# Splitting one chunk's weights pass by pass among the index scores, and another's between the two halves of the inputs

## The reference

```python
h = rmsnorm(x, g_norm_mix[l]) * (1.0 + sc1[:, None, :]) + sh1[:, None, :]
proj = jnp.einsum('bsd,de->bse', h, w_in)          # 4688 columns
qa, ka, va, qi, ki, wi, qb, kb, vb, gb = jnp.split(proj, cuts, axis=-1)
...
# index scores of the sparse attention, 16 heads of 64
dots = jnp.einsum('bqhe,bse->bqhs', qib, k_idx, preferred_element_type=jnp.float32)
score = jnp.einsum('bqh,bqhs->bqs', wb.astype(jnp.float32), jax.nn.relu(dots * IDX_DIM ** -0.5))
_, sel = lax.top_k(score, k_top)                   # 256 keys of each query
...
y_b = retention(qb, kb, vb, gb, positions)         # the second group of heads
```

## Time and profile before

| what | value |
|---|---|
| time, median of 3 runs | 1697.28 us (1694.88 to 1703.69) |
| profiled execution, its own time | 1695.42 us |
| its span, first to last instruction | 1693.5 us |
| PE busy | 1473.0 us, 87% of the span |
| DVE, ACT, POOL busy | 1128.7, 913.3, 279.7 us |
| mean granted TensorE clock | 0.930 |

### The profile page before, as it was taken

How to read it: one execution, slowest core, us unless ns; L and a number is a source line. 1 busy time by engine, 2 the same in 40 slices (tenths; PEclk the granted TensorE clock), 3 DMA queues, 4 the chain that set the end, 5 groups by cost and what they waited for, 6 DMA issues and landing times.

```text
span 1693.5 us, 21565 instructions
## 1 busy us (share of the span) xinstructions
PE 1473.0 (87%) x7406; PEld 1150.1 (68%) x7406; DVE 1128.7 (67%) x1500; ACT 913.3 (54%) x1228; POOL 279.7 (17%) x208
## 2 busy tenths in 40 slices
PE   3899998999999898888899943999999999999940
PEld 2587444888887786456666732788888888888830
DVE  6632778662257983434444345899999999999936
ACT  4320576878994112323444401777777777777711
POOL 0000100240000000200000001223232232332126
PEclk9899989999999998689999966999999999999975
DMA  9198532223324234112211105999999999999847
GB/s 370 50 332 313 200 147 106 90 77 120 109 92 131 69 118 169 65 62 65 86 51 44 38 25 193 401 396 398 404 404 396 394 399 399 394 396 401 347 165 275
DMA packets 102566, 368.01 MB, mean 217 GB/s; under 512 B 11232, under 2 KB 23648, under 8 KB 77792
## 3 DMA queue, kind: packets, MB, share of 16 engines
q1 hardware_dynamic: 74208, 291.58, 45.1%
q10 hardware_dynamic: 17024, 41.95, 6.5%
q0 software_dynamic: 11264, 33.57, 5.5%
HBM read 306.24 MB, written 69.21 MB: 222 GB/s over the span
## 4 chain that ended last, share of the span: by engine, by line
PE 75%; DVE 12%; ACT 4%; issue 3%; DMA 3%; POOL 3%; SPq 0%; DVEq 0%; POOLq 0%; ACTq 0%
PE PS L1627 19%; PE PS L1629 19%; PE PS L1628 19%; PE PS L1728 3%; PE PS L1751 2%; PE PS L1931 2%; PE PS L1837 2%; PE PS L1824 2%; DMA WK<-in_w_ada 1%; DVE wlo L1550 1%; POOL raw L741 1%; DVE WK L1049 1%; PE PS L1713 1%; PE PS L1684 1%; PE PS L1906 1%
## 5 line engine op out<-in xcount | busy, mean ns | idle before, releaser
L1550 DVE TENSOR_TENSOR wlo<-raw,whi 128x2048 fp32r<-128x2048 f32 x192 | 435.8, 2285 | 33.4 <-ACT whi L962 32.9
L962 ACT ACTIVATE whi<-raw 128x2048 fp32r<-128x2048 f32 x192 | 363.9, 1914 | 116.2 <-DVE WK L1569 80.7
L1627 PE MATMUL PS<-whi,xhi 128*128 128x512 f32 x512 | 203.6, 398 | 7.3 <-DVE wlo L1550 6.5
L1629 PE MATMUL PS<-whi,xlo 128*128 128x512 f32 x512 | 200.9, 392 | 0.0
L1628 PE MATMUL PS<-wlo,xhi 128*128 128x512 f32 x512 | 199.9, 390 | 0.0
L853 ACT ACTIVATE KV<-ACC,WK 128x1024 int8<-128x1024 f32 (+4 forms) x160 | 147.5, 925 | 29.9 <-DVE WK L1185 27.3
L1627 PE MATMUL PS<-KVR,BIGR 128*128 128x512 f32 x320 | 127.6, 399 | 5.9 <-DVE KVR L1111 5.9
L1629 PE MATMUL PS<-KVR,BIGR 128*128 128x512 f32 x320 | 125.4, 392 | 0.0
L1628 PE MATMUL PS<-KVR,BIGR 128*128 128x512 f32 x320 | 125.0, 391 | 0.0
L702 POOL COPY wcol<-tw 128x1 f32 (+1 forms) x32 | 63.0, 1970 | 373.9 <-DVE WK L1587 373.9
L1627 PEld LDWEIGHTS PS<-whi,xhi 128*128 128x128 f32 x512 | 96.9, 189 | 27.6 <-issue 5.7
(11 more groups left out here) (326 smaller groups left out, 2966.0 us busy)
## 6 DMA issues: line engine op xcount, KB each, us to landing
raw<-in_w_gate SPq DMA_DIRECT2D x64, 1024.0 KB, 7.2
raw<-in_w_up SPq DMA_DIRECT2D x64, 1024.0 KB, 7.8
raw<-in_w_down SPq DMA_DIRECT2D x64, 1024.0 KB, 7.2
y_dram<-zero ACTq DMA_DIRECT2D x8, 3072.0 KB, 11.3
WK<-in_w_ada POOLq DMA_DIRECT2D x16, 1024.0 KB, 7.4
y_dram<-WK ACTq DMA_DIRECT2D x32, 512.0 KB, 6.6
KV<-in_w_in SPq DMA_DIRECT2D x5, 2048.0 KB, 10.4
KV<-in_x SPq DMA_DIRECT2D x16, 512.0 KB, 5.2
```

What stands on the lines that cost most here:

```text
L962: nc.scalar.activation(whi[:, slot], raw[:, q], ACT.Copy).then_inc(G("m_hi"), 1)
L1550: V.tensor_tensor(wlo[:, slot], raw[:, q], whi[:, slot].bitcast(F32), ALU.subtract)\
L1627: mm(out_, x_hi, w_hi, start=first, stop=False)
L1629: return mm(out_, x_lo, w_hi, start=False, stop=final)
```

## The change

Chunk 0's high passes on ACT now stand between the copy of the first keys and `hidden_high(1)`. Chunk 2's high passes are put one each behind the relus of u = 48, 52, 56 and 60; its low passes on DVE one each ahead of the sums of u = 50, 54, 58 and 62, each behind the wait for that unit's relu. The block of four low passes behind the memsets is gone. No instruction is added or taken out, and PE, POOL and SP have the orders they had.

```diff
--- before.py
+++ after.py
@@ -35,6 +35,7 @@
 TBL = MAX_ITEMS + 2
 NEG_SCORE = -3.0e38
 
+SPLIT_AT = 4
 STEP_SPEND = 5.0
 TAKEN = -3.4e38
 NEG_LOGIT = -1.0e30
@@ -783,11 +784,11 @@
 
 
 
-            def split_high(n):
+            def split_high(n, part=None):
 
                 act.wait_ge(G(f"ld_w{n % 3}"), 16 * (n // 3 + 1))
                 raw_, _, hi = W[n]
-                for k in range(0, KD, 2):
+                for k in range(0, KD, 2) if part is None else (2 * part,):
                     own.go(A(hi[:, k:k + 2], raw_[:, k:k + 2], ACT.Copy), G("w_hi"))
 
             def hidden_high(half):
@@ -815,10 +816,10 @@
             hidden_high(0)
             act.wait_ge(G("key_pe"), 1)
             own.go(A(keys_turned[0:KEYS, 0:512], PS[0:KEYS, 6, :], ACT.Copy), G("key_act"))
+            split_high(0)
             hidden_high(1)
             act.wait_ge(G("key_pe"), 2)
             own.go(A(keys_turned[0:KEYS, 512:1024], PS[0:KEYS, 7, :], ACT.Copy), G("key_act"))
-            split_high(0)
             act.wait_ge(G("key_pe"), 3)
             own.go(A(keys.rearrange("p (b t) c -> p b t c", b=2),
                      PS[:, 6:8, 0:4 * KEYS].rearrange("p b (t c) -> p b t c", t=4), ACT.Copy), G("key_act"))
@@ -837,8 +838,8 @@
                     act.wait_ge(G("sc_acc"), u - 2)
                 own.go(A(WA["R"][:, u % 3, 0:K], PS[:, b:b + 2, :].rearrange("p b c -> p (b c)")[:, 0:K], ACT.Relu),
                        G("sc_relu"))
-                if u == NU // 2:
-                    split_high(RETAIN)
+                if u >= NU // 2 and u % SPLIT_AT == 0 and u < NU // 2 + 4 * SPLIT_AT:
+                    split_high(RETAIN, (u - NU // 2) // SPLIT_AT)
 
             for group in range(2):
                 act.wait_ge(G("late_used"), LATE_STEPS)
@@ -1103,10 +1104,10 @@
                 v = tmp.rearrange("p (h c) -> p h c", h=8)[:, :, 0:16].rearrange("p h (a d) -> p h a d", a=2)
                 own(rotate_part(v, t, 8), G("a_rot"))
 
-            def split_low(n):
+            def split_low(n, part=None):
 
                 raw_, lo, hi = W[n]
-                for k in range(0, KD, 2):
+                for k in range(0, KD, 2) if part is None else (2 * part,):
                     dve.wait_ge(G("w_hi"), 4 * n + k // 2 + 1)
                     own.go(V.tensor_tensor(lo[:, k:k + 2], raw_[:, k:k + 2], hi[:, k:k + 2].bitcast(F32), ALU.subtract),
                            G("w_lo"))
@@ -1154,6 +1155,8 @@
                 acc = ACC[:, ACC_OFF[i]:ACC_OFF[i] + K]
                 R = WA["R"][:, u % 3, 0:K]
                 dve.wait_ge(G("sc_relu"), u + 1)
+                if u >= NU // 2 + 2 and (u - 2) % SPLIT_AT == 0 and u < NU // 2 + 2 + 4 * SPLIT_AT:
+                    split_low(RETAIN, (u - 2 - NU // 2) // SPLIT_AT)
                 if h == 0:
                     own(V.tensor_scalar(acc, R, wsc[:, i, h:h + 1], None, ALU.mult), G("sc_acc"))
                 else:
@@ -1168,8 +1171,6 @@
             own(V.memset(sel_flip, 0))
             for group in range(2):
                 own(V.memset(sel_try[:, 3 * group:3 * group + 3], -2 ** 31), G(f"sel_try{group}"))
-            split_low(RETAIN)
-
             def narrow(n):
 
                 bit, group = 31 - n // 2, n % 2
```

## The result

The changed kernel takes 1682.64 us (median of 6 runs, 1681.62 to 1686.32) where the kernel before takes 1697.82 (median of 6, 1694.88 to 1703.69) in the same comparison. The ratio is 0.9909 with a 95% interval from 0.9894 to 0.9924, so 15.2 us are gained, from 12.9 to 18.0 by the interval. The forecast was 1684.9 and a gain of 12.4. In a later comparison the same kernel gave 0.9923 [0.9906, 0.9941], 13.1 us. The forecast range holds both medians; the second interval includes the forecast gain, the first just doesn't.

The account below looks back on a forecast made before the run. The prediction took PE to bound the kernel (75% of the chain that ended last, DVE 12%), with three waits for weight passes. Its terms 2.9 + 3.0 + 6.5 = 12.4 us gave 1697.3 - 12.4 = 1684.9 us, range 1679 to 1693.

Parts of the forecast that it names:

- start: Before unit 0: PE's first split product starts at about 66.4 instead of 69.31, 2.9 us gained.
- tile K = 768: In the scores: DVE's sums take 20.6 instead of 23.6 us despite four added low passes, 3.0 us gained.
- end of PE's scores to first rotation: At unit 16: PE idles 1.1 instead of 5.9 us; 6.5 us gained, 4.7 from the start, 1.75 from the clock.
- a wait of 1.1 us keeps the clock: Ahead of unit 16: full clock assumed, as it was 1.00 after 2.98 us idle before unit 0; worth 1.75 us.
- Rival 1: In the scores: PE's clock falls all the same, 4.3 us lost, gain 8.1, time 1689.2; chance 0.12.
- Rival 2: Around 510: ACT's counts hold PE up later, unit 16's 6.5 come back, gain 5.9, time 1691.4; chance 0.12.
- from 290 to 505 PE without a gap: Sign of being right, behind unit 16: PE stays busy from 290 to 505 us, so the earlier start is kept.
- Rival 3: In the scores: PE, waiting longer for DVE, stays at low clock; 21 us slower, 1718; chance 0.05.
- Rival 4: Low passes wait for ACT's passes and the start's shift is eaten; only 6.5 us gained, 1690.8; chance 0.05.
- The base: Starting time of the forecast: 1697.3 us, the median of the runs shown, 1.9 above the profiled execution's 1695.42.

Follow-up runs that it names:

- start only: Against the kernel before, only chunk 0's high passes moved ahead of the inputs' second half, chunk 2's passes left where they were: 1693.66 us, ratio 0.9976.
- filled waits: The kernel before with no split moved, plus extra matmuls of ones by zeros at PE's three waits: 1690.44 us, ratio 0.9952.
- each half: Against the kernel before, only chunk 0's high passes moved: 1693.66 us, ratio 0.9976; only chunk 2's passes dealt out: 1687.61 us, ratio 0.9943.
- low passes only: Against the kernel before, only chunk 2's low passes dealt out among the sums, its high passes still one block behind u = 48: 1692.53 us, ratio 0.9975.

## Why the prediction was right, and where its sizes were off

The mechanism was the forecast one at all three places; one term was mis-sized. Means over three traces each of before and of the change:

| term | forecast | measured, and its marks |
|---|---|---|
| start | 2.9 | 4.5: scores' first product at 169.88, 173.31, 169.88 against 166.65, 166.37, 166.46 |
| tile K = 768 | 3.0 | 3.4: 23.6, 23.9, 23.8 against 20.3 |
| end of PE's scores to first rotation | 6.5 | 6.3: 13.1, 13.3, 13.2 against 7.0 |
| sum | 12.4 | 14.2; the first rotation itself moved 14.7 (292.05 to 277.35) |

- **The start.** Passes, keys' copy, second low half: each stands within 0.3 us of the forecast. The sizing failed in one sentence, which took only the wait's length; the clock behind it, read as 1.00 in one trace, falls in half of the traces. It costs 1.2 us in the mean of six (1.0 in the three of this table), which fits the 4.0 of start only. The rest of the 4.5 is small: PE's keys end 0.3 us earlier in the mean, and the first product is drawn 0.3 inside them. This is most of the difference between 12.4 and 14.2.
- **The same row was also used as evidence** that a wait of 1.1 us keeps the clock. The conclusion held (1.00 in every trace of a kernel with the short wait), its argument did not: 2.98 us are not safe.
- **The tile.** 20.6 forecast, 20.3 measured. That low passes cost DVE 4.8 in a tile that it paces was booked rightly; their net cost is 3.5 there and 2.4 at the end of PE's scores. PE now ends its scores 36.3 us behind the tile, where before it was 37.1; this 0.8, less 0.3 of scatter ahead of the tile, is what lies between the 14.7 of the rotation and the 14.2 of the terms. The first rival's price for the low clock, 4.3, was measured as 4.2 to 4.5 by the filled waits.
- **Rival 1** (the clock falls all the same) did not come: 1.00 over the whole stretch in the three traces of the change. In the first one ACT waits 0.24 us for DVE at most units of the tile, but PE has only two gaps from 213 to 271, of 0.26 and 0.63 us. The Trainium skill, "TensorE: Matmul & The Clock Gate", section "A second HAM failure mode: psum-queue depth-cycling", describes a clock that swings where TensorE cycles through its PSUM banks and idles briefly between groups of matmuls; no run here shows it at this pace of 1.05 to 1.35 us a unit.
- **Rival 2** (the counts hold PE up later) did not come: PE's wait ahead of L1660/L1661 in the retention is 2.30 before and 2.29 after, 12.9 us earlier. The prediction's "from 290 to 505 PE without a gap" holds but for 0.65 us at 500.81, which before had too, at 513.70. **Rival 3** needs the low clock, and there is none. **Rival 4** is out: DVE does not idle once among its passes, and each half gains by itself.
- **The base.** The forecast stood on the median of runs. The profiled execution of before was one in which the clock held at unit 0; that this is part of why the median lies 2 us above it is likely, with a fall in half of the traces, and not shown run by run. That the clock at unit 0 is all of the spread of before was not tested.

What stays open is whether the 15.2 us by the medians of the first comparison hold something beyond the 14.2 to 14.7 of the traces; both intervals hold the latter, so there need be nothing. Which part of the filled waits' 8.2 us belongs to which place was only read from one trace: 4.3 and 1.5 with the 1.2 of the start make 7.0.

## What to carry to other kernels

Price a wait of the matrix engine with what follows it: after a stall of about three microseconds the same matmuls may run at half speed for several more, and one trace does not tell whether they will, so look at two or three. Work of a helper engine that must be done before a stage is cheapest where that engine waits for something else anyway (here behind the w_ada products), next best spread so thinly that the buffers between the engines bridge each piece, and dearest as a block ahead of the stage. Where a stall can't be removed, throw-away matmuls that end before it does get back the clock's share of it: here 7.7 us by the medians without touching the schedule.

## What the runs showed of the hardware

- A PE idle time of 2.98 us before unit 0 was followed by the low clock in 3 of 6 traces, one of 2.92 us in the scores in all five traces that have it, one of 5.9 us ahead of unit 16 in every trace, and one of 1.1 us there in none of seven.
- Behind the scores' stall the low clock lasted 9 us of steady work in the three traces of before, but less in two others (start only, low passes only): there the three units took 4.54 us instead of 5.48, and the products behind them 1.92 instead of 3.6.
- Matmuls of ones by zeros held the clock: all three places are at 1.00 in the one trace of the filled kernel. At the scores' stall and at unit 16 the clock was low in every trace that has the wait and no such matmuls; at unit 0 half of the traces hold 1.00 anyway, so there this one trace shows little.
- The clock's chance is not bound to the places of the change: behind the same wait of 18.45 us the routing's products took 5.49 to 5.54 us in ten traces and 6.79 to 7.08 in three.
